# Compressed keys and values in one kernel: the gathered blocks as stationary operand, and what is moved around them

## The reference, cut to what matters

```python
h  = modulate_pre(x, kv_norm_g, shift, scale)            # RMS norm, scale and shift
kv = (h @ kv_w).reshape(B, S, 3, 2, G, dh)               # 3 branches, k and v, G = 4 groups, dh = 64
n_cmp  = (S - 32) // 16 + 1                              # 15 windows of 32 tokens, 16 apart
tok    = arange(n_cmp)[:, None] * 16 + arange(32)[None, :]
blocks = kv[0][:, :, :, tok] + cmp_pos                   # (k and v, group, window, token, dh)
blocks = blocks.reshape(2, B, G, n_cmp, 32 * dh)
hid    = gelu(einsum('kbgnf,kfh->kbgnh', blocks, cmp_w1))  # 2048 -> 256 for 4 * 15 = 60 rows
kv_cmp = einsum('kbgnh,khd->kbgnd', hid, cmp_w2)           # 256 -> 64
```

## Time and profile before

| | us |
|---|---|
| median of the 3 runs shown | 2142.9 |
| lowest, highest | 2139.66, 2146.96 |
| span of the profiled execution, first to last instruction | 2136.1 |
| TensorE busy in that span | 2079.7 (97%) |
| VectorE, ScalarE, GpSimd busy | 1556.6 (73%), 1036.3 (49%), 205.3 (10%) |
| second group of `kv_w` done to the start of ffn10's j = 1 | 551.93 to 619.21 |

### The profile page before, as it was taken

How to read it: one execution, slowest core, us unless ns; L and a number is a source line. 1 busy time by engine, 2 the same in 40 slices (tenths; PEclk the granted TensorE clock), 3 DMA queues, 4 the chain that set the end, 5 groups by cost and what they waited for, 6 DMA issues and landing times.

```text
span 2136.1 us, 39424 instructions
## 1 busy us (share of the span) xinstructions
PE 2079.7 (97%) x16970; PEld 2037.4 (95%) x16970; DVE 1556.6 (73%) x1941; ACT 1036.3 (49%) x1169; POOL 205.3 (10%) x334
## 2 busy tenths in 40 slices
PE   5999999999999999999999999999999999999998
PEld 5999999999999998799998999999999999999998
DVE  6878898787857878788877365767888545757554
ACT  3544646445533446663355454355455444346443
POOL 1111101110101101011110100010111000001000
PEclk9999999999889999999999999999999999999999
DMA  8898566995769963169956554456995555545663
GB/s 296 299 331 314 203 231 217 330 345 206 253 219 331 348 232 110 50 231 332 338 203 197 188 183 168 159 186 245 371 385 188 192 188 181 174 158 188 207 214 123
DMA packets 265389, 497.40 MB, mean 233 GB/s; under 512 B 17152, under 2 KB 146560, under 8 KB 264832
## 3 DMA queue, kind: packets, MB, share of 16 engines
q1 hardware_dynamic: 230192, 366.42, 50.4%
q0 software_dynamic: 35024, 128.47, 16.0%
HBM read 491.68 MB, written 1.05 MB: 231 GB/s over the span
## 4 chain that ended last, share of the span: by engine, by line
PE 85%; DVE 8%; ACT 3%; DMA 3%; issue 1%; SPq 0%; POOL 0%; DVEq 0%; ACTq 0%
PE PA L526 8%; PE PA L528 8%; PE PA L527 8%; PE PB L526 8%; PE PB L528 8%; PE PB L527 8%; PE PY L526 7%; PE PY L528 7%; PE PY L527 7%; DVE wlo L1488 2%; PE PA L611 1%; PE PY L559 1%; ACT whi L1093 1%; PE PY L561 1%; PE PY L566 1%
## 5 line engine op out<-in xcount | busy, mean ns | idle before, releaser
L1488 DVE TENSOR_TENSOR wlo<-raw,whi 128x2048 fp32r<-128x2048 f32 x335 | 767.7, 2301 | 336.2 <-ACT whi L1093 335.1
L1093 ACT ACTIVATE whi<-raw 128x2048 fp32r<-128x2048 f32 x329 | 627.1, 1912 | 495.5 <-DMA raw<-ffn_w_in 203.8
L526 PE MATMUL PY<-opB_hi,whi 128*128 128x256 f32 x1344 | 378.6, 282 | 7.3 <-DVE wlo L1488 7.3
L528 PE MATMUL PY<-opB_hi,wlo 128*128 128x256 f32 x1344 | 375.8, 280 | 0.0
L527 PE MATMUL PY<-opB_lo,whi 128*128 128x256 f32 x1344 | 375.8, 280 | 0.0
L526 PE MATMUL PA<-opA_hi,whi 128*128 128x256 f32 x1312 | 370.5, 282 | 3.9 <-DVE wlo L1488 3.9
L528 PE MATMUL PA<-opA_hi,wlo 128*128 128x256 f32 x1312 | 369.3, 282 | 0.0
L527 PE MATMUL PA<-opA_lo,whi 128*128 128x256 f32 x1312 | 368.2, 281 | 0.0
L526 PE MATMUL PB<-opA_hi,whi 128*128 128x256 f32 x1184 | 333.9, 282 | 0.8 <-DVE wlo L1488 0.8
L528 PE MATMUL PB<-opA_hi,wlo 128*128 128x256 f32 x1184 | 333.1, 281 | 0.0
L527 PE MATMUL PB<-opA_lo,whi 128*128 128x256 f32 x1184 | 332.0, 280 | 0.0
(11 more groups left out here) (331 smaller groups left out, 3472.0 us busy)
## 6 DMA issues: line engine op xcount, KB each, us to landing
raw<-ffn_w_in SPq DMA_DIRECT2D x176, 512.0 KB, 5.8
scr<-adat POOLq DMA_DIRECT2D x160, 512.0 KB, 6.5
raw<-w_in SPq DMA_DIRECT2D x144, 512.0 KB, 4.5
raw<-w_ff SPq DMA_DIRECT2D x128, 512.0 KB, 4.8
raw<-ffn_w_out SPq DMA_DIRECT2D x88, 512.0 KB, 5.2
adaw<-adat POOLq DMA_DIRECT2D x80, 512.0 KB, 6.3
raw<-w_branch SPq DMA_DIRECT2D x48, 512.0 KB, 4.1
raw<-a_w_in SPq DMA_DIRECT2D x24, 512.0 KB, 4.6
```

What stands on the lines that cost most here:

```text
L526: nc.tensor.matmul(o_, w1, rhs(xh), start=start, stop=False, skip_group_check=True)
L528: return nc.tensor.matmul(o_, w2_, rhs(xh), start=False, stop=stop, skip_group_check=True)
L1093: AC(whi[slot][:, 0:w], raw[slot][:, 0:w], ACT.Copy).then_inc(hi_ready, 1)
L1488: TT(wlo[slot][:, 0:w], raw[slot][:, 0:w], whi[slot][:, 0:w].bitcast(F32), ALU.subtract).then_inc(lo_ready, 1)
```

## The change

- **Products of the compression.** Not the weight tile but the blocks are stationary: 65 columns (15 windows of each of 4 groups, four columns in between that are not used, and the position term as the last), read from `eh` and `el` with a step of 8 elements. The weights move, 256 columns at a time. A chunk is 24 matmuls instead of 48. The result stands with rows on partitions (65 x 256 for k, and for v), so ScalarE copies it to `hraw`, TensorE transposes it back (four times), VectorE takes the position column to `pbias`, and gelu adds it as bias.
- **Half-swap.** The 8 matmuls with the selection matrix and the gathering additions are gone. Two transfers on SyncE's queue copy `kvc` with its partition halves exchanged to `kvs`; even and odd tokens are split straight from `kvc` and `kvs` into `eh` and `el` (`split_high` on ScalarE, `split_low` on VectorE, two of each from `kvc` and two from `kvs`).
- **Third group at once.** Chunks c+4 and c+5 follow c+3 directly, into PA and PB.
- **ffn10's input** goes to an operand "C" of its own. GpSimd makes `x * rstd` (8 operations) and `* A + B` (8 operations), ScalarE copies the high parts (`high10`), VectorE makes the low parts (`low10`), between the other work of the stage.
- **The small end**: the four transposes stand behind ffn10's first chunk, `kcmp` and `vcmp` behind its second, in PY.
- **Slabs**: the 12 of this stage (`cmp`) are run in ffn01 (44 for 40) and in ffn10 (52 for 44).

```diff
-        for _name, _count, _run in (... ("ffn01", 40, 40), ("cmp", 0, 12),
-                                    ("ffn10", 24, 44), ...
+        for _name, _count, _run in (... ("ffn01", 40, 44), ("cmp", 0, 0),
+                                    ("ffn10", 24, 52), ...
...
# SyncE
                     chunk(CH["cmp"] + 2 * kv + h, src_in256(I["cmp_w1"][kv], 0, 8 * h))
+                    if kv == h == 0:
+                        need(sp, "S", "kv0")
+                        for u in range(2):
+                            sp.dma_start(kvs[64 * u:64 * u + 64], kvc[64 - 64 * u:128 - 64 * u]).then_inc(kv_swapped, 16)
...
# TensorE
-                for g in range(GROUPS):
-                    last = nc.tensor.matmul(PS[buf][:, g, :], selu[:, g % 2, :], kvc[:, 2 * kv + g // 2, :],
-                                            start=True, stop=True)
...
-            zgroup(CH["kv"] + 4, "Y", tile_in512, "kv")
+            zgroup(CH["kv"] + 4, "AB", tile_in512, "kv")
...
+            need(pe, "V", "elo")
...
-                        for m in range(2):
-                            last = mm3(PA[:, 2 * kv + m, 0:60], c % RING, tile_in256(k, m), (bh, bl),
+                        wh, wl = whi[slot][:, 256 * k:256 * k + 256], wlo[slot][:, 256 * k:256 * k + 256]
+                        xh, xl = (e_[:, kv, kk:kk + 513:8] for e_ in (eh, el))
+                        nc.tensor.matmul(o_, xh, wh, start=kk == 0, stop=False, skip_group_check=True)
+                        nc.tensor.matmul(o_, xh, wl, start=False, stop=False, skip_group_check=True)
+                        last = nc.tensor.matmul(o_, xl, wh, start=False, stop=kk == 15, skip_group_check=True)
...
-            ffn("ffn10", "10", False)
+            ffn("ffn10", "10", False, "C", (hidden_turned, compressed_kv))
...
# ScalarE
+            for hf in range(2):
+                split_high(kvc, hf, hf)
             prep_to(c + 6)
+            for k in range(4):
+                high10(k)
             zcopy("kv1", [kslc[:, 0, :], kslc[:, 1, :], vtmp["slc"][:, 0, :], vtmp["slc"][:, 1, :]])
...
+            prep_to(c + 7)
+            act.wait_ge(cmp_in, 64)
+            S(AC(eh[:, :, 512:528], pos2, ACT.Copy), "epos")
+            act.wait_ge(kv_swapped, 32)
+            for hf in range(2):
+                split_high(kvs, hf, 1 - hf)
+            for k in range(4, KT):
+                high10(k)
+            prep_to(c + 9)
+            zcopy("kv2", [kwin[:, 0, :], kwin[:, 1, :], vtmp["win"][:, 0, :], vtmp["win"][:, 1, :]])
+            prep_to(c + 11)
...
# GpSimd
-            for i in range(6):
-                pool.wait_ge(multiplied, CH["kv"] + 1 + i)
-                ada_send(RUN["cmp"][0] + 2 * i + 2)
+            need(pool, "V", "kv.r")
+            for k in range(KT):
+                S(pool.tensor_tensor(t10[:, k, :], x[:, k, :], rstd[:], ALU.mult), f"10.x{k}")
+            for k in range(KT):
+                need(pool, "G", f"10.x{k}")
+                S(pool.tensor_scalar(t10[:, k, :], t10[:, k, :], A_("10")[:, k:k + 1], B_("10")[:, k:k + 1], ALU.mult, ALU.add), f"10.t{k}")
```

More of the change, by code:

```diff
@@ L317, in build @@
         ADA0, RUN, _n = {}, {}, 0
-        for _name, _count, _run in (("first", 16, 16), ("ffn00", 24, 40), ("conv", 24, 8), ("ffn01", 40, 40), ("cmp", 0, 12),
-                                    ("ffn10", 24, 44), ("nsa", 32, 0), ("ffn11", 40, 40), ("ff0", 48, 48), ("ff1", 8, 8)):
+        for _name, _count, _run in (("first", 16, 16), ("ffn00", 24, 40), ("conv", 24, 8), ("ffn01", 40, 44), ("cmp", 0, 0),
+                                    ("ffn10", 24, 52), ("nsa", 32, 0), ("ffn11", 40, 40), ("ff0", 48, 48), ("ff1", 8, 8)):
             ADA0[_name] = (_n, _count)
@@ L614, in lo_of, with ffn @@
                 return lambda k: need(pe, "V", f"{tag}.lo{k}")
-            def ffn(name, tag, z):
+            def ffn(name, tag, z, op="A", between=None):
                 c0 = CH[name]
@@ L636, in ffn @@
                         for h in range(2):
-                            chunk(p_ + h, (p_ + h) % RING, PS[buf], tile_ffn_in, range(4 * h, 4 * h + 4), 4, "A", 0, 7,
+                            chunk(p_ + h, (p_ + h) % RING, PS[buf], tile_ffn_in, range(4 * h, 4 * h + 4), 4, op, 0, 7,
                                   lo_of(tag) if j == (2 if z else 0) else None)
+                            if between and j == 0:
+                                between[h]()
                         freed[buf] = (hid_made, h0 + j + 1)
@@ L745, in _ @@
-            take("Y")
-            zgroup(CH["kv"] + 4, "Y", tile_in512, "kv")
-            by("Y", "V", "kv2.z")
-            take("A")
-            bh, bl = (oph["B"][:].rearrange("p a b -> p (a b)"), opl["B"][:].rearrange("p a b -> p (a b)"))
-            for kv in range(2):
-                need(pe, "V", f"blo{kv}")
+            for n_ in "AB":
+                take(n_)
+            zgroup(CH["kv"] + 4, "AB", tile_in512, "kv")
+            for n_ in "AB":
+                by(n_, "V", "kv2.z")
@@ L761, in _ @@
                     last.then_inc(multiplied, 1)
-            by("A", "S", "gelu")
-            take("Y")
             for n_, br in enumerate(("slc", "win")):
@@ L1200, in ffn @@
                     prep_to(p_ + 4)
+                    if name == "ffn10" and j == 0:
+                        need(act, "V", "pbias")
+                        for i in range(4):
+                            S(AC(hidc[:, i // 2, i % 2, :].rearrange("p (g n) -> p g n", g=GROUPS),
+                                 flat["Y"][:, 65 * i:65 * i + 64].rearrange("p (g n) -> p g n", g=GROUPS)[:, :, 0:N_CMP],
+                                 ACT.Gelu_apprx_tanh, bias=pbias[:, i:i + 1]), "gelu")
                     if z and j < 2:
@@ L1308, in _, with split_high, high10 @@
             zcopy("kv0", [kvc[:, m, :] for m in range(4)])
+            def split_high(src, hf, par):
+                return S(AC(by_group(eh)[64 * hf:64 * hf + 64, :, par:4:2, :],
+                            src[64 * hf:64 * hf + 64, :, hf:T:2].rearrange("p (v g) t -> p v g t", v=2), ACT.Copy), f"ehi{hf}{par}")
+            def high10(k):
+                need(act, "G", f"10.t{k}")
+                S(AC(oph["C"][:, k, :], t10[:, k, :], ACT.Copy), f"10.hi{k}")
+            act.wait_ge(steps["S"], S.n)
@@ L1688, in ffn @@
                             need(dve, "S", "csil1")
+                        if j == 0 and name == "ffn10":
+                            need(dve, "T", "hidt")
+                            S(nc.vector.tensor_copy(pbias, flat["Y"][:, 0:260].rearrange("p (i c) -> p i c", i=4)[:, :, 64]), "pbias")
                         some(p_)
@@ L1696, in ffn @@
                     low(j)
+                    if j == 0 and name == "ffn10":
+                        need(dve, "T", "cmpkv")
+                        need(dve, "G", "vpad")
+                        S(nc.vector.tensor_copy(kcmp, flat["Y"][:, 512:572]))
+                        for g in range(GROUPS):
+                            S(nc.vector.tensor_copy(vcmp[32 * g:32 * g + N_CMP, :], flat["Y"][32 * g:32 * g + N_CMP, 320:384]), "vcmp")
             def angles():
```

130 lines of the change are left out of this document (65 added, 65 removed).

## The result

The changed kernel takes 2120.85 us in the median of 4 runs (2119.42 to 2122.36); the kernel before took 2141.28 us in the same session (4 runs, 2139.01 to 2146.96). The ratio is 0.9899, 95% interval 0.9881 to 0.9917: about 20.4 us less, where 23.5 were predicted.

The account below looks back on a forecast made before the run. Bound taken: TensorE's number of stationary tiles in the compression, plus the fallen clock. The stage's 67.3 us become 42.8 (-24.5), slabs +1, total -23.5; span 2112.6 plus 6.8 gives 2119.4 us, likeliest range 2113 to 2125.

Parts of the forecast that it names:

- Pitch of the products: Compression's 96 turned products: 0.119 us each, with 0.43 us as upper bound if strided stationary reads cost double.
- signs of being right: Products 0.12 us apart at clock 1.00, one 3 to 4 us wait at fourth chunk, none at small end, j = 1 24 us earlier.
- signs of being wrong: Starts 0.2 us or more apart, wait ahead of first product, GpSimd's second lot above 1 us each, ffn01/ffn10 waits above 3 us.
- -25.8 us: Compression's products: 96 of 256 moving columns take 11.4 us in place of 37.2 us.
- No wait ahead of the first product: First compression chunk's blocks ready in time, with GpSimd's first 8 products at 0.73 us each ending at 550.3 us.
- The fourth chunk: Compression's fourth chunk, c+9: TensorE waits for its low part until 575.9 us, +3.7 us.
- Clock behind the waits: Clock falls behind the wait at the fourth chunk: +1.7 us, with 0 and 3 us as ends.
- Small end, gelu, half-swap: Transposes and small products 2.9 us; gelu no longer holds TensorE; half-swap transfers cost 0, there by about 554 us.
- Slabs: 12 slabs moved into ffn01 and ffn10: +1 us, ends 0 and 2.7.
- GpSimd is slow: Rival, chance 0.13: GpSimd's two-scalar operation at 2.6 us makes c+9's low part late, +9.5 us, 2129 us.
- forecast of 2112.6: Profiled span after the change, from 2136.1 us less 23.5 us.

Follow-up runs that it names:

- e5: Changed kernel with ffn10's input split late, the third group out of PSUM earlier, and chunk c+9 between VectorE's low parts: 2110.78 us, ratio 0.9858.
- e1: Changed kernel with the compression's products turned back: weights stationary, 64 columns moving with a step of 8, 192 products, position term left out: 2144.5 us, ratio 1.0022.
- e11: Kernel with weights stationary and 192 products, streaming 256 neighbouring columns, other ones than the reference's: 2127.62 us, ratio 0.994.
- e2: Changed kernel with all eight high and low parts of ffn10's input behind the split of the swapped halves: 2115.51 us, ratio 0.9884.
- e7: Changed kernel with GpSimd's two passes undone; VectorE makes x*A*rstd, ScalarE and VectorE add B: 2119.38 us, ratio 0.9893.
- e6: Fastest reordered kernel, with the stationary operand read as 65 neighbouring columns instead of every eighth, other columns than the reference's: 2111.97 us, ratio 0.9868.
- e4: Changed kernel with 14 small products filling TensorE's wait ahead of the first compression product: 2120.71 us, ratio 0.9906.
- e8: The changed kernel itself run again, nothing changed, for comparison on one chip: 2120.86 us, ratio 0.9903.
- e10: Kernel with weights stationary and 192 products, streaming 256 columns, every second one, position term left out: 2145.76 us, ratio 1.0025.
- e9: Kernel with weights stationary and 192 products, streaming 128 columns, every fourth one, position term left out: 2143.38 us, ratio 1.001.
- e12: Kernel with weights stationary and 192 products, streaming 128 neighbouring columns, other ones than the reference's: 2144.02 us, ratio 1.0016.

## Why the prediction came out, point by point

**All runs on one line.** Stretch and median go together over all kernels, 37.9 to 72.6 us: the median less the stretch is 2074.6 us for the change, 2072.9 for e5, 2073.6 for e1, 2074.9 for e11, and between 2072.4 (e2) and 2076.7 (e7) for all. So the large differences between kernels are made in the stage, and what lies around it is the same to some 4 us.

- **Pitch of the products: right.** 0.119 us was taken, 0.126 is measured at the full clock (e5), with 0.43 as the other end. The step accounts for what lies above (e6: 0.117 without it). Of the prediction's signs of being right, the pitch, the one wait at the fourth chunk and the quiet small end came; of its signs of being wrong, one came, the wait ahead of the first product.
- **What the -25.8 us consist of.** It was taken as one term, 37.2 to 11.4; with 12.1 us for 96 turned products (96 x 0.126) it is -25.1. e11 divides it: there 192 products with the weights stationary take 24.5 us, since the clock comes back. Of the 25.1 us, 12.7 (37.2 - 24.5) are then the clock and 12.4 (24.5 - 12.1) the number of products. This is an estimate, as e11 differs from the old products in its moving columns too, and keeps a short low clock at its start.
- **No wait ahead of the first product: wrong, 3.8 us.** The step that failed is the working of GpSimd's row: "at 0.73 us each the 8 products end at 550.3". The price of one was right (four of the eight took 0.73 to 0.74 us). What it left out is that these products stand beside VectorE's subtractions, and the two engines hold each other up: two took 2.8 us and two 1.2, so the eight took 10.6 us instead of 5.9. The second lot made up 0.4 us of this by the fourth result. ScalarE's fourth high part, and with it kv1's storing and all that is queued behind, came 4.5 us late. VectorE's own slowing (0.55 us at chunk c+5) cost nothing on top, since VectorE then waited 2.31 us for the first high part. The view of the kernel before had the sign: GpSimd's sums in place take 0.75 us in the median and up to 2.67 us (its row below). e2 and e7, which take GpSimd off these lists in two ways, both end that wait.

```profile
L2145 POOL TENSOR_TENSOR accx<-accx,tmp x60: 726/746/2672, 43.1 to 1944.9; 128x256 f32<-128x256 f32 x60
```

- **The fourth chunk: right in kind, early by 4.3 us.** It was due 575.9 - 551.9 = 24.0 us behind c+3, and was there after 28.3 us. It is GpSimd's 4.4 us, handed down both lists, and the whole error of the sum, since the first wait ends in this gate's shadow (e4): +4.3 there, and together -0.9 for the last 24 products, the transposes and j = 0 with its small products, 17.9 us (598.96 - 581.04) against 18.8.
- **Clock behind the waits.** 1.7 us were taken, once. The 72 products took 10.7 us where 72 x 0.126 is 9.1, and the last 24 took 4.3 (581.04 to the transposes at 585.36) against 3.0. Of these 2.9 us only the second part, 1.3 us, counted, and in e8 it was not there: its last 24 products behind a wait of 1.5 us took 3.2.
- **Small end, gelu, half-swap: right.** j = 0 with four transposes and the small products takes 598.96 - 586.41 = 12.55 us, 11.45 + 1.6 was taken. No wait stands at them. The half-swap's transfers took 6.2 us to landing, instead of 5.8, from 548.4 us on; the data was there by 555 us, and wanted at 564 (559 in the prediction's working, so it would have been in time there too). Their row among the DMA issues after (size of each, median us to landing):

```profile
mix<-mix SPq DMA_DIRECT2D x2, 256.0 KB, 6.2
```

- **Slabs: +1 taken, 0 measured.** TensorE has no wait for a low part in ffn10, and ffn01 has none that it had not before.
- **GpSimd is slow** was a rival, with 0.13, priced at 2.6 us an operation with two per-partition scalars and +9.5 us. It asked about the right engine and the wrong operation: that one took 0.63 us in the mean. GpSimd's results were late all the same, by the first lot, and the stretch is 3.4 us longer for it. The better questions were what runs beside the operation, and its place in ScalarE's strict list: it stands ahead of kv1's storing, so what it is late by goes straight into the gate.
- **From the stage to the median: partly luck.** The measured change is 20.4 us, 3.1 less than the 23.5 predicted; the stage gained 3.4 less, and the 1 us charged for the slabs was not lost. The median came within 1.5 us because that of the kernel before also fell, from 2142.9 to 2141.28, with a fourth run. The span was 8.0 us above its forecast of 2112.6, since the two profiled executions differ outside the stage: behind j = 1 the program took 1516.9 us before and 1521.6 after, and all profiles lie between 1514.0 (e2) and 1525.0 us (e4). The profile of before was one of its kernel's faster executions: its runs beside the experiments lie 2.0 to 2.2 us above their spans, which makes about 2138.2 us of 2136.1, an estimate, while that of after was the slowest of its four (2122.36).

**What stays open.** Which executions lose time behind the stage. All profiles have the waits of 2.4 us in the earlier trace rows and near 1950 us, but those for low parts between 1480 and 1700 us differ, 2.7 us before, 4.9 after, 1.9 to 4.6 in the others, and why was not tried. And the same wait is followed by a low clock in one profile and not in the next. In the first profile of the change it is at 776, 892, 1552, 1648 and 1952 us, in e8 at 524, 772, 800, 1140 and 1648 us. No run here decides it. What the third group's new place alone is worth, and the turned products alone, was not tried.

## What to carry to other kernels

When an engine works through a strict list, ask for each item how late it may be before the next engine's gate moves, and test by filling or removing the nearer wait: if the total doesn't move, the gate is further down, and two waits in series need both mended (3.1 us each alone, 8.3 together). Turn a product with few moving columns so that the wide side moves, and put the side that is read with a step where it is stationary. Price an operation by the whole spread of its row, not by its least time, and ask for each instruction what the engine beside it runs at that moment: here that, and not the operation, made 5.9 us into 10.6.

## What the runs showed of the hardware

- A step of two float32 on the moving operand doubled the pitch of a product of 256 columns, 0.228 against 0.117 us, at a clock of 1.00 (e10, e11); a step of eight on a stationary operand of 65 columns cost 0.009 us (e5, e6).
- Behind a wait of 3.7 us products of 256 columns got the full clock back (0.60, then 0.97 in the two stretches from 568 us after the change), while products of 64 or 128 columns behind the same wait stayed at 0.50 for 37 to 38 us with TensorE never idle (e1, e9, e12). With the wait filled by small products the clock stayed at 1.00 (e4).
- GpSimd's product of two inputs took 0.73 us for 256 columns where VectorE did not hold it up, about twice VectorE's 0.36 for a subtraction (1.43 for four low parts); its operation with two per-partition scalars took 0.55 at the least and 0.63 in the mean. The Trainium skill, "GPSIMD Engine Reference", section "4.1 Engine selection", has about twice VectorE's time for two inputs, and the rows agree.
- Beside a chunk's subtraction of 2.28 us on VectorE the same product took 2.78 to 2.80 us, in the change (where it ended 0.60 us behind VectorE), e2, e5 and e8. Where GpSimd's product had begun first, VectorE's chunk took 2.83 instead of 2.28 us; over two splits it was 2.01 against 1.41 (e7).
